# Fourteen blocks of products of constants on TensorE in a two-part model on one core

## The reference, cut to what matters

```python
def rmsnorm(x, w):
    xf = x.astype(jnp.float32)
    y = xf * lax.rsqrt(jnp.mean(xf * xf, axis=-1, keepdims=True) + NORM_EPS)
    return (y * w.astype(jnp.float32)).astype(x.dtype)

def modulate(x, norm_w, shift, scale):
    return rmsnorm(x, norm_w) * (1 + scale) + shift
...
x = x + (gate * mix).astype(x.dtype)
shift, scale, gate = adaln(c, dense_mod_w[i], dense_mod_b[i])
ffn = swiglu(modulate(x, dense_norm[i], shift, scale), dense_w_gu[i], dense_w_down[i])
```

## Time and profile before

| | |
|---|---|
| runs | 3119.28, 3113.44, 3119.92 us |
| median | 3119.28 us |
| profiled execution, first to last instruction (span) | 3114.3 us |
| instructions | 51962 |
| PE busy | 2933.0 us (94%), 23528 matrix records and as many weight loads |
| DVE busy | 1225.4 us (39%) |
| ACT busy | 714.7 us (23%) |
| DMA | 687.00 MB, 221 GB/s over the span |
| mean granted TensorE clock | 0.967 |
| chain that ended last | PE 90%, DVE 6%, ACT 3%, DMA 1%, issue 1% |

### The profile page before, as it was taken

How to read it: one execution, slowest core, us unless ns; L and a number is a source line. 1 busy time by engine, 2 the same in 40 slices (tenths; PEclk the granted TensorE clock), 3 DMA queues, 4 the chain that set the end, 5 groups by cost and what they waited for, 6 DMA issues and landing times.

```text
span 3114.3 us, 51962 instructions
## 1 busy us (share of the span) xinstructions
PE 2933.0 (94%) x23528; PEld 2024.0 (65%) x23528; DVE 1225.4 (39%) x2176; ACT 714.7 (23%) x1144; POOL 47.5 (2%) x37
## 2 busy tenths in 40 slices
PE   5898998998999999999999899889999999988898
PEld 5788997877333333333333466689999885687898
DVE  5668853242111101101101277445555443454454
ACT  2224333131000000000000112334333322311343
POOL 0000000000000000000000000000000000032000
PEclk8899999999999999999999999999999999999999
DMA  7756764536899999999999322046566431010452
GB/s 288 290 201 256 286 232 170 196 120 253 327 364 358 364 368 372 356 362 376 366 354 364 135 68 95 1 149 230 217 230 227 166 123 53 1 71 6 165 182 82
DMA packets 96947, 687.00 MB, mean 221 GB/s; under 512 B 10576, under 2 KB 13776, under 8 KB 13904
## 3 DMA queue, kind: packets, MB, share of 16 engines
q1 hardware_dynamic: 94064, 678.47, 56.6%
q10 hardware_dynamic: 2656, 5.14, 0.4%
HBM read 682.52 MB, written 1.05 MB: 219 GB/s over the span
## 4 chain that ended last, share of the span: by engine, by line
PE 90%; DVE 6%; ACT 3%; DMA 1%; issue 1%; POOL 0%; DVEq 0%; ACTq 0%
PE ps L485 40%; PE ps L1942 19%; PE ps L821 11%; PE ps L1965 7%; PE ps L732 6%; PE ps L1968 3%; PE ps L496 2%; PE ps L709 1%; PE ps L1950 1%; DMA XT<-XIN 1%; DVE macc L578 1%; ACT HT L670 1%; DVE FR L802 0%; DVE RN L680 0%; DVE AR L2438 0%
## 5 line engine op out<-in xcount | busy, mean ns | idle before, releaser
L1942 PE MATMUL ps<-AR 128*32 128x512 f32 x4080 | 533.5, 592 | 0.0
L485 PE MATMUL ps<-HT,ring 128*128 128x256 f32 (+1 forms) x1696 | 446.2, 424 | 9.6 <-ACT HT L670 9.6
L485 PEld LDWEIGHTS ps<-HT,ring 128*128 128x128 f32 x1696 | 326.6, 194 | 122.4 <-issue 79.7
L485 PE MATMUL ps<-FR,FR 128*128 128x256 f32 x3120 | 389.9, 285 | 1.7 <-DVE M_moe_mod L587 1.7
L485 PEld LDWEIGHTS ps<-FR,FR 128*128 128x128 f32 x3120 | 379.5, 192 | 11.5 <-issue 9.5
L2053 DVE TENSOR_TENSOR AR<-AR,ps 128x256 f32<-128x256 f32 x84 | 35.5, 423 | 802.1 <-ACT AR L2017 802.1
L821 PE MATMUL ps<-FR,FR 128*128 128x256 f32 x2832 | 349.3, 283 | 0.0
L821 PEld LDWEIGHTS ps<-FR,FR 128*128 128x128 f32 x2832 | 343.9, 192 | 0.8 <-issue 0.8
L1942 PEld LDWEIGHTS ps<-AR 128*32 128x32 f32 x4080 | 150.8, 110 | 297.0 <-issue 294.5
L802 DVE TENSOR_TENSOR FR<-ring,FR 128x2048 fp32r<-128x2048 f32 x129 | 294.4, 2291 | 116.1 <-ACT FR L786 116.1
L786 ACT ACTIVATE FR<-ring 128x2048 fp32r<-128x2048 f32 x129 | 244.6, 1906 | 120.2 <-PE ps L821 92.6
(11 more groups left out here) (411 smaller groups left out, 2603.6 us busy)
## 6 DMA issues: line engine op xcount, KB each, us to landing
ring<-W SPq DMA_DIRECT2D x441, 1024.0 KB, 6.2
AR<-W SPq DMA_DIRECT2D x205, 1024.0 KB, 7.9
XT<-XIN ACTq DMA_DIRECT2D x2, 1024.0 KB, 16.8
cst<-CS ACTq DMA_DIRECT2D x1, 1851.0 KB, 35.7
out<-XT SPq DMA_DIRECT2D x1, 1024.0 KB, 4.5
sml<-SM ACTq DMA_DIRECT2D x1, 986.5 KB, 32.5
cst<-CS ACTq DMA_DIRECT2D x1, 129.5 KB, 7.6
C<-SM ACTq DMA_DIRECT2D x1, 4.0 KB, 5.2
```

The lines of the kernel that those rows point to most:

```text
L485: ins = g.matmul(out, l, r, **kw)
L1942: ins = g.matmul(bank.ap[group(i), :], mo.hg[e % 2][:, 4 * h + k, group(t)], w[n][:, k, :], start=j == 0 and k == 0, stop=j == 1 and k == ...
```

## The change

A helper `warm` is added. It takes the next PSUM bank, waits until it is empty, and issues n products of the identity with 256 columns of the constants into it. Nobody reads the bank afterwards. It is called at thirteen places in the text of the program, one of them in `mlp_pe`, which runs twice: fourteen blocks, 144 products in all. Since nobody signals that such a bank is empty, `wait_emptied` now takes a missing entry as no wait.

```diff
-            for one in self.c.emptied[bank.before]:
+            for one in self.c.emptied.get(bank.before, ()):
...
+        def warm(g, s, name, n):
+
+            b = counts.take("warm", name)
+            s.wait_emptied(b)
+            for _ in range(n):
+                g.matmul(b.ap[:, 0:256], ident, cst[:, 0:256], start=True, stop=True)
+
...
             norm_pe(g, s, "hy")
+            bg.go(2)
+            warm(g, s, "hy0", 6)
             bg.finish("hyb_mod")
+            warm(g, s, "hy1", 8)
             norm_done(s, "hy")
...
             scores(1, 0)
+            warm(g, s, "cmp", 16)
             for j in range(2):
                 compressed(j)
...
         def dense_pe(g, s, bg):
+            warm(g, s, "dense0", 8)
             norm_pe(g, s, "dense")
             bg.finish("dense_mod")
+            warm(g, s, "dense1", 8)
...
             bg.finish("ssm_mod")
+            warm(g, s, "ssm", 12)
...
             bg.finish("moe_mod")
+            warm(g, s, "moe", 12)
...
             bg.finish("ada0")
+            warm(g, s, "rank", 10)
             b = counts.take("mo.rank")
...
+            if p == "mo":
+                warm(g, s, "scatter", 6)
             scatter(7)
...
                 if n == 0:
                     norm_pe(g, s, "even")
+            warm(g, s, "even", 6)
             norm_done(s, "even")
...
             norm_pe(g, s, p)
+            warm(g, s, p, 16)
             s.wait_marks(mlp_before(q)[1], "TVAG")
...
+            warm(g, s, "odd", 10)
             bg.finish("ada1")
...
             even_ctx_pe(g, s)
+            warm(g, s, "fin0", 10)
             norm_pe(g, s, "fin0")
```

## The result

The changed kernel took **3124.55 us** (median of 12 runs, 3118.41 to 3126.17), the kernel before 3116.70 us on the same chip (12 runs, 3113.44 to 3119.92). The ratio is 1.0025, interval 1.0017 to 1.0033: slower by a quarter of a per cent, some 7.8 us. The forecast was 3118.6 us, a gain of 0.7. The time lies in the range of 3108 to 3127, but the sign was wrong: slower by over 0.2% had a chance of 0.16. The forecast started from the median of three executions before, 3119.28 us; that of twelve is 2.6 us lower, so in time alone the miss looks smaller (6.0 us) than it is against the kernel before (8.5 us).

A forecast was written before the change was run, and what follows sets the result against it. The prediction took TensorE, busy 94% of the span, to bound the kernel. Its terms for the blocks summed to -0.7 us, from 3119.28 to 3118.6 us, with a range of 3108 to 3127 us.

The forecast's parts named there:

- fin0: Ten products between the context's and final norm's sums delay ACT's root, its shift and so TensorE: +5.0 us (+2.8 to +5.5).
- even: Block behind the even stage's context products, ahead of 38.56 us without a gap: costs its full length, +2.7 us (to +3).
- ssm: Block of 5.4 us in a wait of 6.65 us ahead of the Mamba stage's first products: -3.0 us.
- hy: Blocks hy0 and hy1, eight products in a wait of 4.40 us, perhaps partly at half clock: -2.5 us (-2.9 to 0).
- odd: Block of 4.5 us in a wait of 5.84 us at the odd stage: -3.1 us (-3.1 to 0).
- cmp: Sixteen products ahead of all four compression slots; TensorE comes sooner and meets the weight transfer: -1.5 us (-3.8 to +1.7).
- dense: Blocks dense0 and dense1 at the dense stage; TensorE merely waits longer ahead of the split products: -0.3 us (-1.7 to +1.7).
- moe and rank: Router: moe speeds it up by 2.1 us, rank's ten products cost beyond 1.9 us spare, clock -0.8: -0.3 us together.
- m0 and m1: Sixteen products ahead of each MLP's split products; the gain becomes a wait on DVE's weight conversion: +1.0 and +1.3 us.
- A: Rival: every half-clock stretch is won and blocks outside their waits cost nothing: 3092.5 us, chance 0.08.
- B: Rival: as forecast, but cmp, hy and the clock behind m0, m1 and rank near their good ends: 3111.6 us, chance 0.2.
- C: Rival: slower, because blocks run at half clock and outgrow their waits: 3127.4 us, chance 0.17.

The follow-up runs named there:

- e4: Only the blocks hy0, hy1, ssm, moe and odd, each directly ahead of a long wait, without bank turns: 3105.73 us, ratio 0.9961 to the kernel before.
- e3: Only the blocks fin0 and even, without bank turns: 3123.49 us, ratio 1.0020 to the kernel before.
- e10: Only cmp, dense0, dense1, rank, scatter and the two MLP blocks (80 products), without bank turns: 3123.28 us, ratio 1.0028 to the kernel before.
- e2: The changed kernel with all fourteen blocks and products, but each block gives its bank's turn back: 3119.78 us, ratio 1.0012 to the kernel before.
- e1: The changed kernel with its fourteen blocks taking their bank turns and waits but issuing no products: 3117.72 us, ratio 1.0005 to the kernel before.
- e9: The changed kernel, bank turns included, without the blocks fin0 and even: 3116.78 us, ratio 1.0000 to the kernel before.
- e5: Only the block fin0, no bank turn, and ACT's shift of the context half moved ahead of the final norm's root: 3117.97 us, ratio 1.0005 to the kernel before.
- e8: The changed kernel, but hy0, hy1, cmp, dense0 and dense1 give their bank turns back: 3121.13 us, ratio 1.0015 to the kernel before.
- e12: e11 without the 12 products ahead of the context's sums and the 14 ahead of the first norm's: 3105.13 us, ratio 0.9963 to the kernel before.
- e11: e7 without cmp, plus 14 products ahead of the first norm's sums, 12 ahead of the context's, 6 ahead of the last scatter: 3104.65 us, ratio 0.9962.
- e7: e4 plus 16 products ahead of the compression's fourth slot, 10 behind the ranking products, 7 behind the final norm's sums: 3104.27 us, ratio 0.9963.

## Why the prediction was wrong

**The sums fit.** By the ratios, e4's blocks are -12.2 us, e3's +6.2, e10's +8.7: together +2.7, where e2, which has them all, measured +3.7. The rest to +7.8, some 4 us, is the turns'; this is a difference of two kernels, and e1, which has the turns alone, measured only +1.6 (-1.2 to +4.4). In the table, measured less forecast is +7.7 us: +3.7 in the rest of the dense stage, +2.0 in Mamba, +1.7 at `fin0`, +1.0 at the compression, and -0.7 in all else.

The forecast's terms for the clock are shares of the (1 - clock) x length of the windows of the earlier trace rows: 2.9 us at 51 us, 4.2 at 137, 3.0 at 474, 3.3 at 784, 1.7 at 1779, 3.0 at 2068 and 3.4 at 2487. These are estimates, and no run shows one of them as such; the runs showed -3.2 us in the place of the first, -2.7 for the third and -2.8 for the last, up to the next wait. Against the forecast's terms:

- **The turns (forecast: no term).** This is the step that failed outright. The three groups of blocks (in their wait, moving work into it, ahead of work without one) were priced by products and waits, and no block as a holder of a bank. The kernel before gives the banks out in turn, so fourteen more holders move every later claim of a bank; one of them, in the dense stage, then lands on a bank that DVE reads only behind 4.50 us of weight conversion. The two kernels' orders show that the wait on DVE's modulation stands 48 products earlier. +3.7 us in the stretch, in the changed kernel and again in e9: 2.02 of wait, the rest half clock (0.79 in 303.73 to 312.00 and 0.80 in 303.49 to 312.00, where e1 shows 1.00).
- **fin0 (+5.0, range +2.8 to +5.5).** The mechanism was right: the block delays ACT's root, hence the shift, hence TensorE, and e5 shows it by taking ACT's order away. The size in the changed kernel was 6.55 us (18.32 to 24.87 from the experts' end), above the upper bound. The difference is ahead of the block, the stop of 1.45 us at 1768.60. e9 has that stop without the block and needs 20.56 us, so the block's own price is 4.3, inside the range, and 2.2 are not its own. Other kernels with the block show 22.5 (e2), 23.7 (e3) and 25.6 us (e8), others without it and with ACT's old order 18.0 to 19.8 (e1, e4, e10).
- **even (+2.7).** +2.6. Right.
- **ssm (-3.0).** The -3.0 of the sum is the whole (1 - clock) x length of its window, which no run shows; the runs showed -2.7 by the next wait (473.96 to 542.88, against 474.29 to 545.91), at a clock of 1.00 in the window 470 to 486. Near enough. But 1.7 of it was lost again up to the router; the window 543 to 548 has a clock of 0.66 now and had 1.00. In e2, with the same products and without the turns, that window shows 0.96, and the whole of Mamba is 3.6 us shorter than before the change. It repeats: the three kernels whose ssm block takes a turn (the changed one, e8, e9) need 295.5 to 295.7 us from Mamba's first products to the router's; of the five where it gives the turn back, four need 293.0 and e12 294.5. So the turn may well cost 2.5 us here too, although no wait of TensorE is longer; how wasn't found. Without the block it is 295.5 to 298.3 us, so a single trace is a rough base.
- **hy (-2.5), odd (-3.1), scatter (0).** -3.2, -2.8, and nothing to be seen. Odd and scatter are right. hy's -3.2 is a little beyond its end of -2.9, by one pair of traces; the eight kernels that have hy0 and hy1 reach the products behind L1273 at 109.3 to 110.9 us, the six that don't at 111.0 to 112.7, which is 2.1 us in the mean.
- **cmp (-1.5) and dense (-0.3).** -0.8 together. The forecast's reason, the collision with the transfer, was not what kept the gain away: the wait at 140.20 us is only 0.65. The clock fell at 133 us (0.57) although the wait there was 1.66 us and sixteen products at full clock (7.17 us) lay before it. In e10 it did not fall (1.00), and the gain was 3.0 us against this trace of the kernel before. But from the products behind L1273 to the split products the kernels with this block need 134.8 to 139.2 us and those without any 136.0 to 140.7, so a gain by the block isn't shown.
- **moe and rank (-0.3).** -0.2: the sum was right. By e4, moe is -2.5 (I had -2.1 of it reach the end, and -0.8 of clock) and rank +2.4.
- **m0 and m1 (+1.0, +1.3).** +0.4 and +1.5; +1.4 and +1.5 in e10. The new wait on L809 (1.93 and 1.94 us) took the place of the gain, and at m1 the half clock behind it the rest (48 records in 7.50 us, clock 0.50 from 2926.0 to 2929.4; at m0 in 6.02). Right in mechanism, and in size within 0.6 us.

**The rivals.** A, that every stretch is won (3092.5), is refuted by e3 and by the MLPs. The clock did rise (0.967 to 0.979), and e4 won time where the filler fits its wait (-12 us), but the changed kernel got slower. B did not come about: hy came out at its good end in this trace, but cmp and the clock behind m0, m1 and rank did not, and the turn cost. C gave 3127.4, near the measurement, but for another reason: only hy1 ran partly at half clock (5.20 us); ssm, cmp, rank and fin0 ran at full clock (7.17 us for sixteen).

**The chances.** Of the 0.16 for slower, 0.12 came from case C and 0.04 from the tail of the forecast's own case. No case stood for a term that had been left out, and the one that was left out, the turn, costs. The forecast allowed 3 us for half-clock stretches that come and go between executions; the twelve executions of e12 spread over 17 us, those of the kernel before over 6.5 and of the changed one over 7.8. For the median that matters less, but a single stretch of one profiled execution, of before or after, can carry some of it: one of 137 us was 3.9 us longer in e12 than in e11, with the same instructions.

**What stays open.** Why the clock falls at 133 us in one kernel and holds in another; why e10 lost 7 us in stages without blocks; what the turn does in Mamba; and whether the turns cost 3 to 4 us in the median or less, since the intervals of the ratios overlap.

## What to carry to other kernels

In these runs a filler on the bounding engine was worth it only where the instruction directly behind it waits, for about that wait, and where the work behind the wait is TensorE's own; there it paid some 2 to 3 us for each of four long waits (-12 us together in e4). Before the MLPs' split products it filled its wait (1.31 us left of 8.22 at the second) and won nothing, since the next wait, on DVE's conversions (1.93 and 1.94 us), took the gain. Ahead of work that doesn't wait it cost its length (`even`, +2.6 us for 2.7), and `fin0` 4.3 us by the traces, because another engine's written order hangs on what it delays: there, moving one step of ACT made the same ten products free. And a filler takes more than time: look at what else it takes a turn of (here a PSUM bank, and a wait of 2.02 us), and compare where each wait stands in both orders before any is called harmless.

## What the runs showed of the hardware

- Executions of one kernel differ in time and in granted clock. The twelve of e12 spread over 17 us, at mean clocks from 0.972 to 0.980, with the same instructions. In the profiled executions of e11 and e12, which have the same instructions from there on up to the experts' end, the stretch from the products behind the wait of 2.46 us (109.55 and 110.35 us) to the dense stage's split products (246.33 and 251.05) is 136.8 and 140.7 us long, at mean clocks of 0.88 and 0.85; (1 - clock) x length is 16.4 and 21.1 us.
- A wait of 1.66 us ahead of 133.77 went with a fallen clock (0.58 in 132 to 144 us), one of 1.36 at 136.39 in e10 with a full one (1.00). The wait of 2.46 us on DVE's AR is the same in all kernels, and the 14 records behind it took 2.07 us before the change (at 112.67) and 1.16 in e10 (at 112.22); the length of a wait alone doesn't tell.
- The clock rows and the lengths of products don't always agree at the very start. The window 30 to 37 us of the kernel before shows a granted clock of 1.00, while the eight norm products in it took 6.60 us, against 3.62 later. ACT's squares aren't the reason for all of it: the last one ends at 32.43 us and the sums at 36.94. In e11, behind fourteen products, the same sums take 3.62 us, so the 6.60 look like half clock that the row doesn't show. They ended only 1.3 us earlier there than in e7, and nothing changed behind.
- The flag, branch and barrier behind the experts stand in the trace of e11 as 5.54 us of issue on TensorE, 2.90 on DVE and 8.89 on ACT. No run separates the three, and a block behind them doesn't fill that time.
